# A decoder trunk on one core: GpSimd computes the low parts of 24 weight units beside the banded attention

## The chip, the cores and the metric

The kernel runs on one core of a Trainium2 chip. The metric is the device time of one launch in microseconds (us). Before the change it is 2423.09 us, the median of 3 runs (2422.06 to 2423.93).

The engines are named as in the profile: PE is TensorE, PEld its weight loads, DVE is VectorE, ACT is ScalarE, POOL is GpSimd, SP is SyncE, which issues the weight loads from memory.

## The reference, cut to what matters

Two decoder layers over 256 tokens of width 2048, in float32. Layer 0 begins with the banded grouped-query attention that the change is about:

```python
def swa_sink_attention(h, w_qkv, w_o, sinks):      # 32 heads of 64, 4 key/value heads, window 128
    q, k, v = split(h @ w_qkv)
    scores = q @ band(k).T * 64 ** -0.5 + alibi_bias, masked to the window
    probs = softmax(concat([scores, sink]))[..., :-1]
    return (probs @ band(v)) @ w_o

for i in range(2):
    h = h + (swa_sink_attention if i == 0 else diff_attention)(rmsnorm(h), ...)
    h = h + mem_cross_attention(rmsnorm(h), rmsnorm(mem), ...)
    h = h + conv_ffn(rmsnorm(h), ...)
return rmsnorm(h)
```

## The kernel before

**Weight units.** All weights stream through the core as 396 units of 512 x 512 numbers, numbered in the order of use. Unit u lies in slot u % 4. Four steps make it ready:

1. SP loads it into `raw` (1 MB); the load waits until the low part of unit u - 4 is done (`lo_ready`).
2. ACT rounds it to fp32r, the high part: `hi_unit`, L215, `whi <- raw`. It waits for the load and until PE has used unit u - 4 (`units_used`), and counts `hi_ready` up.
3. DVE subtracts, the low part: `lo_unit`, L223, `wlo <- raw - whi`. It waits for `hi_ready` and counts `lo_ready` up.
4. PE multiplies by both parts in three matmuls a tile (L309 to L311, `triple`), behind a wait for `lo_ready`, and counts `units_used` up.

`hi_unit` and `lo_unit` run AHEAD = 3 units before PE's use.

**The stage of the change** is `swa_group`, once for each of four groups g of 8 heads. B_SWA = 4, so the attention begins at unit 16. PE uses units 24 to 27 in group 0 (queries of the next group), 28 to 35 in group 1, 36 to 43 in group 2 (queries and output projection by turns), 44 to 47 in group 3 (output projection); the last output block follows with units 48 to 51 (`last_blocks`, and `final_blocks` on DVE and ACT). The high and low parts made in the stage are those of units 27 to 50.

Each engine's order is written out by hand, and each runs its own instructions in that order only. For one head j:

- PE: the scores (L611, L612); in groups 1 and 2 a unit behind every head's scores, in groups 0 and 3 behind those of odd heads only; then the transposes of the probabilities of head j - 1 (L621), then its products with the values for head j - 2 (L632 to L634).
- DVE: first `swa_normalize` of head j - 1 (L1489 sum, L1492 reciprocal, L1494 and L1495 scaling of the probabilities in `pbuf`), which waits for ACT's exponentials; then `swa_bias_max` of head j (L1474 bias, L1478 and L1479 maxima, L1482 negative maximum), which waits for PE's scores; then, where there is output projection, an addition to `h` (L373); then `lo_unit` of a coming unit: in groups 1 and 2 behind every head, in group 0 behind even heads, in group 3 behind odd ones.
- ACT: in the same rhythm first `hi_unit` (L215); in even heads from 4 on the copy of two heads' outputs (L1074); the exponentials of head j (L1063 to L1067), which wait for L1482; the copy of the transposed probabilities of head j - 1 (L1058).

At a group's end DVE also prepares the next group's keys, values, slopes and sinks (L1462 to L1466) and the low part of the outputs (L1500; in group 3 by halves, L1506, whose first half PE's L309 of the last block needs). GpSimd has no arithmetic in this kernel: it fills `ones` once and issues 14 small loads in the first 20 us.

Of the kernel before, what the change touches and what calls it, by code (L numbers as in the profile page):

```python
# [25 lines left out]
F32 = mybir.dt.float32  # L26
F32R = mybir.dt.float32r
ALU = mybir.AluOpType
# [25 lines left out]
SLOTS = 4  # L54
AHEAD = 3
# [3 lines left out]
B_SWA = B_MEM + 2 * DEPTH  # L59
# [3 lines left out]
B_X[1] = B_DIFF + 12 + 4  # L63
B_FF[1] = B_X[1] + 2
UNITS = 4 * (B_FF[1] + 3 * FF_STEPS)


X_MEM = [0, 1]
# [7 lines left out]
def trunk(nc, x, mem, norm_mix, norm_cross, norm_mem, norm_ffn, norm_final,  # L76
# [4 lines left out]
    with ExitStack() as ctx:  # L81
        def sb(name, shape, dt=F32):
            return ctx.enter_context(nc.sbuf_tensor(name, shape, dt))

        def sem(name):
            return ctx.enter_context(nc.semaphore(name))


        raw = sb("raw", [P, SLOTS, 4, 512])
        whi = sb("whi", [P, SLOTS, 4, 512], F32R)  # L90
        wlo = sb("wlo", [P, SLOTS, 4, 512], F32R)
# [67 lines left out]
        hi_ready = sem("hi_ready")  # L159
        lo_ready = sem("lo_ready")  # L160
# [46 lines left out]
        def hi_unit(act, b4, j):  # L207

            if isinstance(b4, int) and 4 * b4 + j >= UNITS:
                return  # L210
# [6 lines left out]
        def lo_unit(dve, b4, j):  # L217

            if isinstance(b4, int) and 4 * b4 + j >= UNITS:
                return  # L220
            s = j % SLOTS
            dve.wait_ge(hi_ready, b4 * 4 + j + 1)
            dve.tensor_tensor(wlo[:, s], raw[:, s], whi[:, s].bitcast(F32), ALU.subtract)\  # L223
               .then_inc(lo_ready, 1)
# [272 lines left out]

        @block.gpsimd
        def _(pool):
            pool.memset(ones[:], 1.0).then_inc(ones_ready, 1)  # L500

            pool.wait_ge(tokens_landed[1], 16)
            pool.dma_start(stage[0:16, P:2 * P], norm_final.rearrange("(c f) -> c f", f=P))\
                .then_inc(consts_landed, 16)
            for l in range(DEPTH):
                c0 = 256 + 4 * l * P
                pool.dma_start(stage[0:88, c0:c0 + 3 * P].rearrange("c (w f) -> c w f", w=3),
                              ffn_conv_w[l].rearrange("w (c f) -> c w f", f=P)).then_inc(consts_landed, 16)
                pool.dma_start(stage[0:88, c0 + 3 * P:c0 + 4 * P],
                              ffn_conv_b[l].rearrange("(c f) -> c f", f=P)).then_inc(consts_landed, 16)  # L510
            pool.dma_start(dist_swa[:], const_dist_swa).then_inc(consts_landed, 16)
            pool.dma_start(dist_diff[:], const_dist_diff).then_inc(consts_landed, 16)
            pool.dma_start(slopes[:], const_slopes).then_inc(consts_landed, 16)
            pool.dma_start(sinks[:], swa_sinks.broadcast_to([P, SWA_HEADS])).then_inc(consts_landed, 16)
            pool.dma_start(subln[:], diff_subln.rearrange("o n -> n o")).then_inc(consts_landed, 16)
            pool.dma_start(lamv[:, 0], diff_lambda_q1.broadcast_to([P, DIFF_DIM])).then_inc(consts_landed, 16)
            for i, a in enumerate((diff_lambda_k1, diff_lambda_q2, diff_lambda_k2)):
                pool.dma_start(lamv[:, 1 + i], a.broadcast_to([P, DIFF_DIM])).then_inc(lam_landed, 16)


        @block.tensor
# [837 lines left out]
        def _(dve):  # L1359
# [94 lines left out]
            def swa_queries(i, done):  # L1454

                dve.wait_ge(units_used, done)
                scaled_by_rstd(dve, q_sb[:, 2 * i:2 * i + 2], PA[:, 512 * i:512 * i + 512], 1,
                               SWA_DIM ** -0.5).then_inc(swa["q_evac"], 1)
# [9 lines left out]
            def swa_bias_max(g, j):  # L1468
                a = j % 2
                n = g * 8 + j  # L1470
                dve.wait_ge(swa["scores"], n + 1)
                if not isinstance(g, int) or 8 * g + j >= 2:
                    dve.wait_ge(swa["pT"], n - 1)
                dve.scalar_tensor_tensor(out=pbuf[:, a, 0:384], in0=dist_swa[:], scalar=slopes[:, j:j + 1],  # L1474
                                         in1=PC[:, 512 * a:512 * a + 384], op0=ALU.mult, op1=ALU.add)\
                   .then_inc(swa["biased"], 1)
                dve.wait_ge(swa["biased"], n + 1)
                dve.tensor_reduce(stat[:, a, 0, 0:1], pbuf[:, a, 0:P], AX_X, ALU.max)  # L1478
                dve.tensor_reduce(stat[:, a, 0, 1:2], pbuf[:, a, P:3 * P], AX_X, ALU.max)\  # L1479
                   .then_inc(swa["maxed"], 1)  # L1480
                dve.wait_ge(swa["maxed"], n + 1)
                dve.tensor_scalar(stat[:, a, 1, 0:2], stat[:, a, 0, 0:2], sinkg[:, j:j + 1], -1.0,  # L1482
                                  ALU.max, ALU.mult).then_inc(swa["negmax"], 1)

            def swa_normalize(g, j):
                a = j % 2
                n = g * 8 + j
                dve.wait_ge(swa["exped"], n + 1)
                dve.tensor_tensor(stat[:, a, 2, 0:2], stat[:, a, 2, 0:2], stat[:, a, 3, 0:2], ALU.add)\  # L1489
                   .then_inc(swa["summed"], 1)  # L1490
                dve.wait_ge(swa["summed"], n + 1)
                dve.reciprocal(stat[:, a, 4, 0:2], stat[:, a, 2, 0:2]).then_inc(swa["recips"], 1)  # L1492
                dve.wait_ge(swa["recips"], n + 1)
                dve.tensor_scalar(pbuf[:, a, 0:P], pbuf[:, a, 0:P], stat[:, a, 4, 0:1], None, ALU.mult)  # L1494
                dve.tensor_scalar(pbuf[:, a, P:3 * P], pbuf[:, a, P:3 * P], stat[:, a, 4, 1:2], None, ALU.mult)\  # L1495
                   .then_inc(swa["p_ready"], 1)

            def o_lo_all(s, g):
                dve.wait_ge(s["o_hi"], g + 1)
                dve.tensor_tensor(olo[:], o_sb, ohi[:].bitcast(F32), ALU.subtract).then_inc(s["o_lo"], 1)  # L1500

            def o_lo_half(s, i):

                part = slice(2 * i, 2 * i + 2)
                dve.wait_ge(s["o_hi"], GROUPS + i)
                dve.tensor_tensor(last_olo[:, part], o_sb[:, part], last_ohi[:, part].bitcast(F32),  # L1506
                                  ALU.subtract).then_inc(s["o_lo"], 1)

            def add_block(s, b4, j, src, nb):

                dve.wait_ge(units_used, b4 * 4 + j + 1)
                add_to_h(dve, src, nb).then_inc(s["h_added"], 1)

            def swa_group(g, with_q, with_o):
                b4 = g * 2 + (B_SWA + 1) if with_o else B_SWA + 2
                if with_o and not with_q:
                    b4 = B_SWA + 7
                src = [PB, PB, PB, PB] if with_q else [PA, PB, PA, PB]
                for j in range(8):
                    if j >= 1:  # L1520
                        swa_normalize(g, j - 1)
                    swa_bias_max(g, j)
                    if with_o and j >= 2 and j % 2 == 0:
                        add_block(swa, b4, j - 1 if with_q else j // 2 - 1, src[j // 2 - 1][:], j // 2 - 1)
                    if with_q and with_o:
                        lo_unit(dve, b4, j + AHEAD)
                    elif j % 2 == (0 if with_q else 1):
                        lo_unit(dve, b4, j // 2 + AHEAD)
                if with_q and with_o:
                    swa_queries(0, b4 * 4 + 7)  # L1530
                if not with_q:
                    o_lo_half(swa, 0)
                swa_normalize(g, 7)
                if not with_o:
                    swa_queries(0, b4 * 4 + 4)
                if with_o:
                    add_block(swa, b4, 7 if with_q else 3, src[3][:], 3)
                if with_q:
                    dve.wait_ge(swa["scores"], g * 8 + 8)
                    swa_queries(1, b4 * 4 + (7 if with_o else 4))  # L1540
                if with_q:
                    dve.wait_ge(swa["pv"], g * 8 + 8)
                    dve.wait_ge(swa["exped"], g * 8 + 8)
                    swa_prepare(g + 1)
                    o_lo_all(swa, g)
                else:
                    o_lo_half(swa, 1)
# [7 lines left out]
            with dve.Fori(1, 3) as g:  # L1555
                swa_group(g, True, True)
            swa_group(3, False, True)

            def add_wide(s, b4, j, p, nb, count):

# [298 lines left out]
            with dve.Fori(1, 3) as g:  # L1859
                b4 = g * 4 + (B_DIFF + 2)  # L1860
# [25 lines left out]
            b4 = B_DIFF + 14  # L1886
# [71 lines left out]
```

## Time and profile before

| | |
|---|---|
| median of 3 runs | 2423.09 us |
| the profiled execution, its own time | 2420.84 us |
| its span, first to last instruction | 2419.3 us |
| granted clock of TensorE, share of full speed | 0.996 |
| busy share PE / PEld / DVE / ACT / POOL | 98 / 88 / 75 / 49 / 0 % |
| low parts on DVE | 396 of 2288 ns, 904.9 us |
| the four groups of the stage, from and to | about 171 to 214, 214 to 278, 278 to 342, 342 to 394 us |

In rows of the trace, a start time in us from the span's start comes first, then a duration in us, the engine, the line, the operation and what it writes and reads. A bracket at the end is idle time of that engine just before, and who ended it.

### The profile page before, as it was taken

How to read it: one execution, taken by the hardware profiler on the slowest of the kernel's cores; microseconds unless marked ns; L12 is line 12 of the kernel's file. 1: busy time of each engine (PE TensorE's matmuls, PEld its weight loads, DVE VectorE, ACT ScalarE, POOL GpSimd, SP SyncE). 2: the span in 40 equal slices, each digit the busy share in tenths (PEclk: the TensorE clock that was granted, in tenths of full speed). 3: DMA queues.
4: the chain of work that ended last, by engine and by line, in shares of the span. 5: the costliest groups of instructions: out<-in, count | busy, mean ns of one | idle time of the engine just before them, and what ended most of it. 6: DMA issues, size and time to landing. Idle time of an engine off the chain costs nothing.

```text
span 2419.3 us, 37209 instructions
## 1 busy us (share of the span) xinstructions
PE 2372.3 (98%) x15166; PEld 2123.1 (88%) x15166; DVE 1805.5 (75%) x2160; ACT 1184.2 (49%) x1362; POOL 8.6 (0%) x19
## 2 busy tenths in 40 slices
PE   6999999999999999999999999999999999999998
PEld 6898889988888888888899989888888888888887
DVE  5766667768787777777966866788778787777777
ACT  5544446654444444444535444456544444444444
POOL 1000000000000000000000000000000000000000
PEclk9999999999999999999999999999999999999999
DMA  7653433465555555555464554434555555555551
GB/s 258 211 175 107 138 116 117 165 204 183 195 188 189 191 191 190 182 198 188 153 215 150 168 174 152 164 137 165 198 187 182 194 188 190 191 191 191 182 199 54
DMA packets 211818, 423.90 MB, mean 175 GB/s; under 512 B 6896, under 2 KB 7184, under 8 KB 211216
## 3 DMA queue, kind: packets, MB, share of 16 engines
q1 hardware_dynamic: 211152, 421.69, 52.1%
q0 software_dynamic: 576, 0.92, 0.2%
q8 instruction: 68, 1.11, 0.2%
q14 instruction: 22, 0.18, 0.0%
HBM read 420.48 MB, written 2.10 MB: 175 GB/s over the span
## 4 chain that ended last, share of the span: by engine, by line
PE 94%; DVE 4%; ACT 1%; DMA 1%; issue 0%; SPq 0%; DVEq 0%; ACTq 0%
PE pair L335 40%; PE pair L337 20%; PE pair L309 10%; PE pair L310 10%; PE pair L311 10%; DVE wlo L223 1%; PE pair L621 1%; PE pair L612 0%; PE pair L632 0%; PE pair L611 0%; DMA raw<-in_x_w_kv 0%; ACT whi L215 0%; DMA raw<-in_mem 0%; PE pair L633 0%; DVE h L1570 0%
## 5 line engine op out<-in xcount | busy, mean ns | idle before, releaser
L223 DVE TENSOR_TENSOR wlo<-raw,whi 128x2048 fp32r<-128x2048 f32 x396 | 904.9, 2288 | 297.5 <-ACT whi L215 297.2
L215 ACT ACTIVATE whi<-raw 128x2048 fp32r<-128x2048 f32 x396 | 756.7, 1913 | 686.8 <-PE pair L337 511.9
L335 PE MATMUL pair<-xx,whi 128*128 128x512 f32 x2944 | 1023.3, 394 | 0.0
L337 PE MATMUL pair<-xx,wlo 128*128 128x256 f32 x2944 | 816.3, 277 | 0.0
L335 PEld LDWEIGHTS pair<-xx,whi 128*128 128x128 f32 x2944 | 552.0, 188 | 129.0 <-issue 0.5
L337 PEld LDWEIGHTS pair<-xx,wlo 128*128 128x128 f32 x2944 | 552.8, 188 | 0.1
L335 PE MATMUL pair<-oo,whi 128*128 128x512 f32 x1280 | 445.1, 394 | 2.5 <-DVE h L1570 2.5
L337 PE MATMUL pair<-oo,wlo 128*128 128x256 f32 x1280 | 354.7, 277 | 0.0
L309 PE MATMUL pair<-xx,whi 128*128 128x256 f32 x1184 | 342.3, 289 | 10.9 <-DVE wlo L223 9.6
L310 PE MATMUL pair<-xx,whi 128*128 128x256 f32 x1184 | 335.9, 284 | 0.0
L311 PE MATMUL pair<-xx,wlo 128*128 128x256 f32 x1184 | 335.9, 284 | 0.0
L335 PEld LDWEIGHTS pair<-oo,whi 128*128 128x128 f32 x1280 | 240.0, 188 | 58.9 <-DVE h L1570 3.1
L309 PEld LDWEIGHTS pair<-xx,whi 128*128 128x128 f32 x1184 | 227.9, 193 | 21.2 <-issue 19.6
L337 PEld LDWEIGHTS pair<-oo,wlo 128*128 128x128 f32 x1280 | 240.3, 188 | 0.0
L310 PEld LDWEIGHTS pair<-xx,whi 128*128 128x128 f32 x1184 | 228.1, 193 | 1.2 <-issue 1.0
L311 PEld LDWEIGHTS pair<-xx,wlo 128*128 128x128 f32 x1184 | 228.0, 193 | 0.0
L309 PE MATMUL pair<-oo,whi 128*128 128x256 f32 x512 | 147.7, 288 | 1.0 <-DVE oo L1500 1.0
L1564 DVE TENSOR_TENSOR h<-h,pair 128x512 f32<-128x512 f32 x176 | 112.9, 683 | 43.2 <-PE pair L337 43.2
L311 PE MATMUL pair<-oo,wlo 128*128 128x256 f32 x512 | 144.9, 283 | 0.0
L310 PE MATMUL pair<-oo,whi 128*128 128x256 f32 x512 | 144.8, 283 | 0.0
L1672 DVE TENSOR_TENSOR work<-pair,work 128x512 f32<-128x512 f32 x88 | 56.7, 686 | 99.9 <-ACT work L1185 99.9
L1185 ACT ACTIVATE work<-pair 128x512 f32<-128x512 f32 x88 | 47.8, 595 | 149.6 <-PE pair L337 149.6
(197 smaller groups left out, 2205.6 us busy)
## 6 DMA issues: line engine op xcount, KB each, us to landing
raw<-in_ffn_w_up SPq DMA_DIRECT2D x176, 1024.0 KB, 5.0
raw<-in_ffn_w_down SPq DMA_DIRECT2D x88, 1024.0 KB, 5.0
raw<-in_diff_w_qkv SPq DMA_DIRECT2D x48, 1024.0 KB, 5.1
raw<-in_swa_w_qkv SPq DMA_DIRECT2D x20, 1024.0 KB, 5.1
raw<-in_x_w_kv SPq DMA_DIRECT2D x16, 1024.0 KB, 6.1
raw<-in_swa_w_o SPq DMA_DIRECT2D x16, 1024.0 KB, 5.1
raw<-in_diff_w_o SPq DMA_DIRECT2D x16, 1024.0 KB, 5.0
raw<-in_x_w_q SPq DMA_DIRECT2D x8, 1024.0 KB, 5.5
```

The costliest lines, as they stand in the source:

```text
L215: act.activation(whi[:, s], raw[:, s], ACT.Copy).then_inc(hi_ready, 1)
L223: dve.tensor_tensor(wlo[:, s], raw[:, s], whi[:, s].bitcast(F32), ALU.subtract)\
L309: pe.matmul(dst, ahi, bhi, start=start, stop=False, skip_group_check=True)
L310: pe.matmul(dst, ahi, blo, start=False, stop=False, skip_group_check=True)
L311: return pe.matmul(dst, alo, bhi, start=False, stop=stop, skip_group_check=True)
L335: pe.matmul(banks[m], whi[:, s, k, w], act2[:, c].rearrange("p a t -> p (a t)"), start=c == 0, stop=False, skip_group_check=True)
L337: ins = pe.matmul(banks[m][:, 0:SEQ], wlo[:, s, k, w], act2[:, c, 0], start=False, stop=last and k == 3, skip_group_check=True)
L621: ins = pe.transpose(pt_ps[:, dst_cols], src[:, src_cols], ident[:])
L1185: ins = act.activation(u_sb[:, 2 * i:2 * i + 2], src, ACT.Copy)
L1564: ins = dve.tensor_tensor(part, part, p[i][:].rearrange("p (m a t) -> p m a t", m=2, a=2)[:, :, 0], ALU.add)
L1672: ins = dve.tensor_tensor(part, high, part, ALU.add)
```

## The change

The 24 calls of `lo_unit` in DVE's `swa_group` are gone. GpSimd computes the same 24 low parts, each as soon as the high part is there. The first waits until DVE has done the low parts of all units before 27, which keeps the count `lo_ready` in order, and DVE waits for GpSimd's last one before it goes on with `final_blocks`. The tiles, the loads, and the orders of PE, ACT and SP stay as they are.

```diff
+SWA_UNITS = (4 * (B_SWA + 2) + AHEAD, 4 * (B_SWA + 8) + AHEAD)
...
         @block.gpsimd
         def _(pool):
+            def lo_unit_during_attention(u, j):
+                pool.wait_ge(hi_ready, u + 1)
+                pool.tensor_tensor(wlo[:, j], raw[:, j], whi[:, j].bitcast(F32), ALU.subtract)\
+                    .then_inc(lo_ready, 1)
+
...
+            pool.wait_ge(lo_ready, SWA_UNITS[0])
+            for u in range(*SWA_UNITS):
+                lo_unit_during_attention(u, u % SLOTS)
...
                     if with_o and j >= 2 and j % 2 == 0:
                         add_block(swa, b4, j - 1 if with_q else j // 2 - 1, src[j // 2 - 1][:], j // 2 - 1)
-                    if with_q and with_o:
-                        lo_unit(dve, b4, j + AHEAD)
-                    elif j % 2 == (0 if with_q else 1):
-                        lo_unit(dve, b4, j // 2 + AHEAD)
...
             swa_group(3, False, True)
+            dve.wait_ge(lo_ready, SWA_UNITS[1])
```

On DVE, the first head of group 0 before, from its bias to its probabilities; names are tiles, and in brackets stands what an instruction waits for:

```order
L1474 SCALAR_TENSOR_TENSOR pbuf<-dist_swa,slopes,pair 128x384 [waits swa_scores]
L1478 TENSOR_REDUCE stat<-pbuf 128x1 [waits swa_biased]
L1479 TENSOR_REDUCE stat<-pbuf 128x1
L1482 TENSOR_SCALAR stat<-stat,sinkg 128x2 [waits swa_maxed]
L223 TENSOR_TENSOR wlo<-raw,whi 128x2048 [waits hi_ready]
L1489 TENSOR_TENSOR stat<-stat 128x2 [waits swa_exped]
L1492 RECIPROCAL stat<-stat 128x2 [waits swa_summed]
L1494 TENSOR_SCALAR pbuf<-pbuf,stat 128x128 [waits swa_recips]
L1495 TENSOR_SCALAR pbuf<-pbuf,stat 128x256
```

The same place now (lines of the changed file are 11 higher here):

```order
L1485 SCALAR_TENSOR_TENSOR pbuf<-dist_swa,slopes,pair 128x384 [waits swa_scores]
L1489 TENSOR_REDUCE stat<-pbuf 128x1 [waits swa_biased]
L1490 TENSOR_REDUCE stat<-pbuf 128x1
L1493 TENSOR_SCALAR stat<-stat,sinkg 128x2 [waits swa_maxed]
L1500 TENSOR_TENSOR stat<-stat 128x2 [waits swa_exped]
L1503 RECIPROCAL stat<-stat 128x2 [waits swa_summed]
L1505 TENSOR_SCALAR pbuf<-pbuf,stat 128x128 [waits swa_recips]
L1506 TENSOR_SCALAR pbuf<-pbuf,stat 128x256
```

Nothing stands between the negative maximum and the sum any more; the low part has gone from DVE's row. This is the end of GpSimd's row, behind its last small load:

```order
L525 DMA lamv<-in_diff_lambda_k 128x64
L504 ISA
L504 TENSOR_TENSOR wlo<-raw,whi 128x2048 [waits hi_ready,lo_ready]
L504 TENSOR_TENSOR wlo<-raw,whi 128x2048 [waits hi_ready] x23
L83 UNCONDITIONAL_BRANCH
```

The 24 low parts stand there one behind the other, preceded by one instruction that the compiler adds. The rows of PE, ACT and SP hold the same instructions in the same order as before.

In this text lines have the numbers of the kernel before, for the changed kernel too.

## Rows read from the trace of the kernel before

**Rows 1.** The profile's part 1: busy us, share of the span, instructions

```profile
PE 2372.3 (98%) x15166; PEld 2123.1 (88%) x15166; DVE 1805.5 (75%) x2160; ACT 1184.2 (49%) x1362; POOL 8.6 (0%) x19
```

**Rows 2.** Windows of groups 0 and 1: width, busy PE, PEld, DVE, ACT, POOL, clock

```profile
171.00:214.00 43.00, 39.78 (x300) 34.44 (x296) 28.70 (x75) 22.64 (x59) 0.00 (x0) 1.00 0.35 117
214.00:278.00 64.00, 63.11 (x488) 57.88 (x488) 43.01 (x83) 30.02 (x62) 0.00 (x0) 1.00 0.41 132
```

**Rows 3.** Groups of DVE instructions, 165 to 394 us: busy us, mean ns

```profile
L223 DVE TENSOR_TENSOR wlo<-raw,whi 128x2048 fp32r<-128x2048 f32 x25 | 57.1, 2285 | 3.7 <-ACT whi L215 3.7
...
L1479 DVE TENSOR_REDUCE stat<-pbuf 128x1 f32<-128x256 f32 x32 | 13.1, 408 | 0.0
L1495 DVE TENSOR_SCALAR pbuf<-pbuf,stat 128x256 f32<-128x256 f32 x32 | 11.1, 348 | 0.0
L1494 DVE TENSOR_SCALAR pbuf<-pbuf,stat 128x128 f32<-128x128 f32 x32 | 9.2, 288 | 1.1
```

**Rows 4.** Timeline, group 0, heads 0 and 1

```profile
169.84 1.91 ACT L215 ACTIVATE whi<-raw 128x2048 fp32r<-128x2048 f32 x1 [3.84 <-PE pair L311]
171.65 0.61 DVE L1474 SCALAR_TENSOR_TENSOR pbuf<-dist_swa,slopes,pair 128x384 f32<-128x384 f32 x1 [0.42 <-PE pair L612]
...
172.94 0.23 DVE L1482 TENSOR_SCALAR stat<-stat,sinkg 128x2 f32<-128x2 f32 x1
...
175.28 0.16 DVE L1489 TENSOR_TENSOR stat<-stat 128x2 f32<-128x2 f32 x1
...
176.14 0.61 DVE L1474 SCALAR_TENSOR_TENSOR pbuf<-dist_swa,slopes,pair 128x384 f32<-128x384 f32 x1
...
179.90 0.55 PE L621 MATMUL pair<-ident,pbuf 128*128 128x128 f32 x3 [1.15 <-DVE pbuf L1495]
```

**Rows 5.** Timeline, group 0, between heads 3 and 4

```profile
188.78 1.90 ACT L215 ACTIVATE whi<-raw 128x2048 fp32r<-128x2048 f32 x1
189.94 0.55 PE L621 MATMUL pair<-ident,pbuf 128*128 128x128 f32 x3
...
190.59 0.38 ACT L1074 ACTIVATE work<-pair 128x256 f32<-128x256 f32 x1
...
191.11 0.40 PE L632 MATMUL pair<-ptbuf,work 128*64 128x128 f32 x2 [0.62 <-ACT work L1074]
```

**Rows 6.** Timeline, group 0, heads 6 and 7

```profile
199.50 1.90 ACT L215 ACTIVATE whi<-raw 128x2048 fp32r<-128x2048 f32 x1
...
202.05 0.23 DVE L1482 TENSOR_SCALAR stat<-stat,sinkg 128x2 f32<-128x2 f32 x1
...
210.52 0.55 PE L621 MATMUL pair<-ident,pbuf 128*128 128x128 f32 x3
```

**Rows 7.** Timeline, group 3, head 1

```profile
346.37 1.90 ACT L215 ACTIVATE whi<-raw 128x2048 fp32r<-128x2048 f32 x1
348.64 0.23 DVE L1482 TENSOR_SCALAR stat<-stat,sinkg 128x2 f32<-128x2 f32 x1
...
351.98 0.55 PE L621 MATMUL pair<-ident,pbuf 128*128 128x128 f32 x3 [0.92 <-DVE pbuf L1495]
```

**Rows 8.** Timeline, group 3, head 3

```profile
354.84 1.90 ACT L215 ACTIVATE whi<-raw 128x2048 fp32r<-128x2048 f32 x1
356.75 0.23 DVE L1482 TENSOR_SCALAR stat<-stat,sinkg 128x2 f32<-128x2 f32 x1
...
362.03 0.55 PE L621 MATMUL pair<-ident,pbuf 128*128 128x128 f32 x3
```

**Rows 9.** Timeline, end of group 3

```profile
379.45 0.68 DVE L1506 TENSOR_TENSOR xx<-work,xx 128x512 fp32r<-128x512 f32 x1
...
381.29 0.38 PE L309 MATMUL pair<-xx,whi 128*128 128x256 f32 x1
```

**Rows 10.** Groups of POOL instructions, whole span: busy us, mean ns

```profile
L500 POOL MEMSET ones<- 128x128 f32 x1 | 0.2, 205 | 0.3 <-POOLq L1947 0.3
L1947 POOL MEMSET const-float32-0.0<- 128x1 f32 x1 | 0.1, 99 | 0.3 <-issue 0.3
```

## The prediction

> **What bounds the kernel now.** I read the page's busy shares first: PE works for 98% of the span and DVE for 75% [rows 1]. So DVE's time counts only where PE stands still for it. The windows of the stage come next: in group 1 PE is busy for 63.11 of 64 us, while in group 0 it misses 3.2 us of 43 [rows 2]. Taking 24 x 2.285 = 54.8 us from DVE [rows 3] therefore cannot give 54.8 us back. The timeline shows what it can give: twice, at the opening of group 0 and of group 3, PE's transposes (L621) wait for the scaled probabilities (L1495) of head 1, 1.15 and 0.92 us [rows 4, 7]. Elsewhere in the two groups PE waits for ACT (0.62 us before L632) [rows 5] or for the group's preparation, which the change leaves alone.
>
> The reader should see the rhythm. From the bias of head 1 (176.14) to its transpose (179.90) pass 3.76 us; 1.29 of them lie before L1482 (171.65 to 172.94 in head 0) and 2.47 behind it [rows 4]. In groups 1 and 2 a head takes 64 / 8 = 8 us, and its probabilities are transposed only behind the next head's scores and unit, so 8 us of lateness are hidden there. In groups 0 and 3 every second head has no unit behind its scores, and the probabilities of the odd head before it are wanted almost at once. There the sum is made.
>
> **What the change does.** It removes 24 subtractions from DVE. Between L1482 and the sum (L1489) of a head with a unit, DVE spent 2.2 us on one; without it L1489 starts as soon as the exponentials are done, 1.47 us after L1482 (the 2.47 less about 1.0 from L1489 to the transpose, 0.86 of which lie between L1489 and the next bias, 175.28 to 176.14). In head 0 that is 172.94 + 1.47 = 174.4, not 175.28 [rows 4]: 0.9 us earlier. The same holds in group 3. Both places together would give PE 1.8 us, and no others wait for DVE's low part.
>
> It adds 24 subtractions on GpSimd, each starting when ACT's rounding ends. No row shows GpSimd at arithmetic. The lower bound is DVE's 2.29 us [rows 3]. For the upper one, a fill of 128 columns takes 205 ns and of one column 99 [rows 10], so 0.83 ns a column; three such passes over 2048 columns (two reads, a write) and 0.1 make 5.2 us. I take 4.6: twice DVE's time, since a slower engine that fetches its two operands in turn needs two of DVE's passes; it lies near the upper row, which is the only one of this engine. The Trainium skill (GPSIMD Engine Reference, section 3.1) gives 4497 ns for this size against 2293 ns on DVE; with it the sum below would be 0.8 us smaller, and the second figure agrees with DVE's row.
>
> Speed alone costs nothing: 4.6 us is less than a head's 8 us, PE needs a low part three units later, and the next load into the slot is wanted by ACT only after PE has used the unit, so these cover it. DVE's new wait in front of `final_blocks` is covered too: GpSimd's last unit starts near 377 and ends near 382, and DVE has work until then; behind the wait stand the additions to `h`, which wait for PE's last units.
>
> **The cost that decides is whether DVE can work while GpSimd does.** No row shows it: GpSimd is idle in every window. What speaks for trouble is the way DVE's small instructions reach SBUF. L1495 does 128 more columns than L1494 in 60 ns, 0.47 ns a column, where the subtraction needs 1.12 [rows 3]. So scaling uses two ways into SBUF at once, and a two-operand sum reads two tensors at once. If GpSimd's way is DVE's second, then an instruction of either kind (L1482, L1489, L1494, L1495, L1506) that comes while a 4.6 us subtraction runs stands until its end. The Trainium skill says just this (SBUF — State Buffer, "Who interferes with whom"): the pair of ports is locked for a whole instruction, and DVE instructions in a two-port mode or with two SBUF inputs contend with a GpSimd instruction that reads SBUF. By it the change costs time; without it, it gains 1.8 us. No run here has tested it. Against it stands that PE and ACT read SBUF beside DVE with no visible cost. I take the held case as likelier.
>
> **The sum, held case.**
> - Group 0, opening: the rounding ends at 171.75, GpSimd holds until 176.4. L1482, at 172.94 before, runs at 176.4. The next bias follows 2.35 behind it, at 178.75, and head 1's transpose 3.76 later, at 182.5 instead of 179.90 [rows 4]: +2.6.
> - Heads 2 and 3: exponentials of head 1 end at 181.5, a copy (0.4) and the rounding (1.9) follow, GpSimd works from 183.85 to 188.45. L1482 of head 2 comes at the same moment; I let it slip through. L1489 waits to 188.45, the bias of head 3 follows 0.86 later, its transpose at 193.05. PE wants it at 189.94 [rows 5] + 2.6 = 192.55: +0.5.
> - The next rounding follows head 3's exponentials, at 192.05 + 0.4, so the output copy L1074 starts at 194.3 instead of 190.59, and PE's L632 at 194.8 instead of 191.11 [rows 5]: 3.7 late, +0.6 more.
> - Heads 6 and 7: rounding ends at 201.40 + 3.7, GpSimd holds to 209.7. L1482 wanted 202.05 + 3.7, runs at 209.7; bias 212.05, transpose 215.8 against 210.52 + 3.7 = 214.2 [rows 6]: +1.6. Heads 4 and 5 fit.
> - Group 3, opening: rounding ends 348.27, GpSimd holds to 352.9; L1482 from 348.64 to there, transpose 2.47 later at 355.4 against 351.98 [rows 7]: +3.4.
> - Heads 3 and 5: rounding ends at 356.74 and L1482 starts at 356.75, so I let L1482 through; L1489 waits to 361.4, the transpose comes at 362.4 against 362.03 [rows 8]: +0.35 each.
> - The end: by the same pattern GpSimd's last unit ends 2.3 us behind the old start of L1506, 379.45; that takes 0.68, and PE's L309 wants it at 381.29 [rows 9]. 379.45 + 2.3 + 0.7 = 382.4: +1.1.
>
> Together 5.3 + 5.2 = 10.5 us. PE is the bound behind the stage too, so it is not given back. On the profiled execution's 2420.84 that makes 2431.3; the median stands 2.25 above that execution, so I forecast 2433.
>
> The bounds: with 2.29 us on GpSimd only the openings cost, 0.3 + 1.1, 2424.5. With 5.2 us each of the eight terms grows by 0.6: 15 us, 2438. If the coincidences (L1482 against GpSimd's start) all fall the other way, four terms grow by about 1.5: 17 us, 2440.
>
> **The rivals.**
> - *No interference* (the other side): DVE works beside GpSimd untouched, PE gets its 1.8 us, 2421.3, which a measurement can't tell from no change (0.2% is 4.8 us). It decides if L1482 to L1495 keep their distances while GpSimd works. For it speaks that nothing in the trace shows a hold. 0.27.
> - *Only two-operand instructions are held.* Then L1482 passes, and L1489 waits from 175.28 to 176.4 (+1.1), the later heads of group 0 add 1.0, group 3's opening 1.9 (352.9 less 351.0), the rest 1.8: 5.8 us, 2429. 0.12.
> - *GpSimd becomes the bound.* It needs over 8 us a unit in groups 1 and 2, at 12 us it falls behind by 16 x 4 = 64 us, of which three units ahead hide about 16: 2471. The upper row speaks against it. 0.05.
> - The held case has 0.56. That the change would not do what it says is excluded by the order of instructions.
>
> **How the numbers follow.** Nothing I found gives more than 1.8 us, so faster by over 0.2% has 0.03. Within 0.2% lie the rival without interference and the cheap ends of the others (a fast GpSimd): 0.34. Slower 0.63. The range reaches from the rival without interference to the lost coincidences, 2420.5 to 2440; outside stay the bound GpSimd, dearer holds and a larger gain, some 0.15. The likeliest case's own range is 2426 to 2440.
>
> **What would show it.** In the changed profile: GpSimd's low parts of about 4.6 us, start to start no nearer than a head; in group 0 head 0's L1482 or what follows it starting at GpSimd's end near 176.4, or right after the maxima if I am wrong; PE's waits for L1495 at the two openings grown to 3 to 4.5 us (held) or gone (free); groups 1 and 2 still 64 us each; no wait of DVE for `lo_ready` behind group 3. The prediction is wrong if DVE's instructions keep their starts while GpSimd works, if a GpSimd unit is near 2.3 us or above 8, or if GpSimd is the one that waits and DVE never does.

## The result and the profile after

The changed kernel takes 2439.22 us (median of 4 runs, 2435.65 to 2441.95) against 2422.57 us (4 runs). The ratio is 1.0072, 95% interval 1.006 to 1.0084: 17.4 us slower, between 14.5 and 20.4; the medians differ by 16.7. The forecast was 2433 us, with 10.5 us in its sum and a range up to 2440; 1.0072 times the 2423.09 it started from is 2440.5. One execution of e10, an experiment below, took 13357.5 us and is left out of its numbers.

Rows of the changed kernel and of the experiments have the line numbers of their own files. From the page of the changed kernel: the span, the busy shares, the start of the chain that ended last, by line, and the group of GpSimd's subtractions (out and in, count, busy us, mean ns).

```profile
span 2437.8 us, 37205 instructions
PE 2383.4 (98%) x15166; PEld 2132.1 (87%) x15166; DVE 1840.9 (76%) x2136; ACT 1182.4 (49%) x1362; POOL 119.0 (5%) x43
...
PE pair L337 39%; PE pair L339 20%; PE pair L311 10%; PE pair L312 10%; PE pair L313 10%; DVE wlo L225 1%; DVE stat L1493 1%; PE pair L632 1%; PE pair L623 0%; PE pair L622 0%; PE pair L643 0%; DMA raw<-in_x_w_kv 0%; DMA raw<-in_mem 0%; DVE h L1578 0%; DVE pbuf L1485 0%
...
L504 POOL TENSOR_TENSOR wlo<-raw,whi 128x2048 fp32r<-128x2048 f32 x24 | 110.4, 4599 | 268.9 <-ACT whi L217 268.9
```

DVE lost 24 subtractions of 2.29 us, 55 us, and yet is busy for 1840.9 us, where [rows 1] has 1805.5. The groups of DVE's instructions between 165 and 410 us tell where most of the missing 90 us came from. L1493 is the negative maximum (L1482 before), L1500 the sum (L1489), L1485 the bias (L1474), L1506 and L1505 the two scalings (L1495 and L1494).

```profile
L1493 DVE TENSOR_SCALAR stat<-stat,sinkg 128x2 f32<-128x2 f32 x32 | 66.0, 2062 | 1.1
L1500 DVE TENSOR_TENSOR stat<-stat 128x2 f32<-128x2 f32 x32 | 26.5, 828 | 27.2 <-ACT stat L1078 26.1
L1485 DVE SCALAR_TENSOR_TENSOR pbuf<-dist_swa,slopes,pair 128x384 f32<-128x384 f32 x32 | 19.5, 610 | 8.7 <-PE pair L623 8.7
L1506 DVE TENSOR_SCALAR pbuf<-pbuf,stat 128x256 f32<-128x256 f32 x32 | 15.6, 486 | 0.0
L1505 DVE TENSOR_SCALAR pbuf<-pbuf,stat 128x128 f32<-128x128 f32 x32 | 9.2, 287 | 1.1
```

The negative maximum takes 2062 ns on average, where it takes 229 in the kernel before. In all, L1493, L1500 and L1506 take 84.7 us more than the 7.3, 5.0 and 11.1 us of before. A held instruction is shown as a long one. In the stage 14 of L1493 and 7 of L1500 begin while a subtraction runs, and each of them ends 0.01 to 0.03 us behind that subtraction's end. The bias, with one operand from PSUM, keeps its 610 ns. The opening of group 0 in the order of time, which answers to [rows 4]:

```profile
170.20 1.91 ACT L217 ACTIVATE whi<-raw 128x2048 fp32r<-128x2048 f32 x1 [3.84 <-PE pair L313]
...
172.26 4.62 POOL L504 TENSOR_TENSOR wlo<-raw,whi 128x2048 fp32r<-128x2048 f32 x1 [153.30 <-ACT whi L217]
...
173.30 3.60 DVE L1493 TENSOR_SCALAR stat<-stat,sinkg 128x2 f32<-128x2 f32 x1
...
179.14 0.55 PE L632 MATMUL pair<-ident,pbuf 128*128 128x128 f32 x3 [1.22 <-DVE pbuf L1506]
...
181.76 0.16 DVE L1500 TENSOR_TENSOR stat<-stat 128x2 f32<-128x2 f32 x1 [1.24 <-ACT stat L1078]
```

The maximum starts at 173.30 and ends at 176.90, as the subtraction does (176.88). Head 1's transposes, which started at 179.90 [rows 4], start at 182.76. The opening of group 3, against [rows 7]:

```profile
357.40 4.54 POOL L504 TENSOR_TENSOR wlo<-raw,whi 128x2048 fp32r<-128x2048 f32 x1 [10.14 <-ACT whi L217]
357.71 4.25 DVE L1493 TENSOR_SCALAR stat<-stat,sinkg 128x2 f32<-128x2 f32 x1
...
364.20 0.90 PE L632 MATMUL pair<-ident,pbuf 128*128 128x128 f32 x3 [4.08 <-DVE pbuf L1506]
```

The maximum is held to 361.96; PE waits 4.08 us in place of 0.92. And the transposes themselves take 0.90 us in place of 0.55: PE has become slower. The windows show it (width, busy PE, PEld, DVE, ACT, POOL, then the granted clock, DMA share, GB/s):

```profile
182.00:184.00 2.00, 1.24 (x5) 0.91 (x6) 1.90 (x7) 1.90 (x2) 0.02 (x1) 0.51 0.03 8
184.00:192.00 8.00, 8.00 (x35) 7.02 (x34) 5.38 (x10) 2.72 (x11) 4.52 (x1) 0.50 0.26 77
360.00:364.00 4.00, 0.12 (x1) 0.00 (x0) 2.69 (x5) 1.55 (x6) 1.94 (x1) 0.87 0.17 32
364.00:372.00 8.00, 7.80 (x31) 6.49 (x32) 7.25 (x14) 3.35 (x7) 2.96 (x1) 0.50 0.30 115
```

In the course of both waits the granted clock falls, and TensorE runs for about ten microseconds at 0.50, its lower level of 1.2 GHz; both windows of [rows 2] have 1.00. For head 2's transposes, the next mark behind them, and for the first scores of group 3 the two kernels have these rows, first before, then after (with two more marks, of head 7 in group 0 and of the end of group 3):

```profile
187.87 0.49 PE L621 MATMUL pair<-ident,pbuf 128*128 128x128 f32 x3
...
341.90 0.50 PE L611 MATMUL pair<-work 64*128 64x128 f32 x4 [0.86 <-issue]
...
359.96 0.49 PE L621 MATMUL pair<-ident,pbuf 128*128 128x128 f32 x3
```

```profile
194.98 0.49 PE L632 MATMUL pair<-ident,pbuf 128*128 128x128 f32 x3
...
218.59 0.55 PE L632 MATMUL pair<-ident,pbuf 128*128 128x128 f32 x3
...
350.97 0.50 PE L622 MATMUL pair<-work 64*128 64x128 f32 x4 [0.85 <-issue]
...
376.17 0.49 PE L632 MATMUL pair<-ident,pbuf 128*128 128x128 f32 x3
...
398.84 0.39 PE L311 MATMUL pair<-xx,whi 128*128 128x256 f32 x1 [0.78 <-DVE xx L1517]
```

With them the whole loss can be laid out; each line is the lateness at a mark of PE's row, and what was added since the mark before:

| mark | before | after | late by | added, and by what |
|---|---|---|---|---|
| group 0, head 1 transposed | 179.90 | 182.76 | 2.86 | 0.35 from before the stage (the first bias at 172.00, not 171.65), 2.5 wait |
| head 2 | 187.87 | 194.98 | 7.11 | 4.25, the clock |
| head 7 | 210.52 | 218.59 | 8.07 | 0.96, waits of heads 5 and on |
| group 3, first scores | 341.90 | 350.97 | 9.07 | 1.0, groups 1 and 2 |
| head 1 transposed | 351.98 | 364.20 | 12.22 | 3.15, wait |
| head 2 | 359.96 | 376.17 | 16.21 | 4.0, the clock |
| end of group 3 | 381.29 | 398.84 | 17.55 | 1.3, waits |

The waits make 8.95 us, the clock 8.25. The rest of the kernel adds little: the spans differ by 18.5 us in these two executions.

The 1.0 us of groups 1 and 2 is nearly all one wait, at the end of group 1. The negative maximum of head 7 is held for 4.41 us, and behind this head no further scores follow in its group that would give PE work for the time:

```profile
277.12 4.41 DVE L1493 TENSOR_SCALAR stat<-stat,sinkg 128x2 f32<-128x2 f32 x1
```

```profile
283.77 0.55 PE L632 MATMUL pair<-ident,pbuf 128*128 128x128 f32 x3 [0.91 <-DVE pbuf L1506]
```

Two subtractions can also follow each other closely, and the second then holds another instruction of the same head. Here that cost nothing that PE's waits show, since the head's 8 us hide it:

```profile
239.78 4.60 POOL L504 TENSOR_TENSOR wlo<-raw,whi 128x2048 fp32r<-128x2048 f32 x1 [3.50 <-ACT whi L217]
239.84 1.22 DVE L375 TENSOR_TENSOR h<-h,pair 128x1024 f32<-128x1024 f32 x1
...
241.18 3.22 DVE L1500 TENSOR_TENSOR stat<-stat 128x2 f32<-128x2 f32 x1
...
244.83 4.78 DVE L1506 TENSOR_SCALAR pbuf<-pbuf,stat 128x256 f32<-128x256 f32 x1
244.85 4.61 POOL L504 TENSOR_TENSOR wlo<-raw,whi 128x2048 fp32r<-128x2048 f32 x1 [0.48 <-ACT whi L217]
```

Here too it is seen what is not held: the addition to `h` (L375), whose second operand is in PSUM, takes its 1.22 us in the middle of a subtraction.

### The profile page after: what moved, and what is told of

The parts are those of the page before. It is cut to its first block, busy times and chain, and to the rows that moved or that the text cites. A ratio compares the mean times of both kernels' runs of the same rounds, so it can differ in the third digit from the quotient of the medians.

```text
span 2437.8 us, 37205 instructions
## 1 busy us (share of the span) xinstructions
PE 2383.4 (98%) x15166; PEld 2132.1 (87%) x15166; DVE 1840.9 (76%) x2136; ACT 1182.4 (49%) x1362; POOL 119.0 (5%) x43
## 4 chain that ended last, share of the span: by engine, by line
PE 92%; DVE 5%; ACT 1%; DMA 1%; issue 1%; SPq 0%; DVEq 0%; ACTq 0%
PE pair L337 39%; PE pair L339 20%; PE pair L311 10%; PE pair L312 10%; PE pair L313 10%; DVE wlo L225 1%; DVE stat L1493 1%; PE pair L632 1%; PE pair L623 0%; PE pair L622 0%; PE pair L643 0%; DMA raw<-in_x_w_kv 0%; DMA raw<-in_mem 0%; DVE h L1578 0%; DVE pbuf L1485 0%
## 5 line engine op out<-in xcount | busy, mean ns | idle before, releaser
L225 DVE TENSOR_TENSOR wlo<-raw,whi 128x2048 fp32r<-128x2048 f32 x372 | 850.0, 2288 | 297.6 <-ACT whi L217 297.3
L504 POOL TENSOR_TENSOR wlo<-raw,whi 128x2048 fp32r<-128x2048 f32 x24 | 110.4, 4599 | 268.9 <-ACT whi L217 268.9
```

Source lines behind the costliest of these rows:

```text
L504: pool.tensor_tensor(wlo[:, j], raw[:, j], whi[:, j].bitcast(F32), ALU.subtract)\
```

## The experiments

Theory A: a GpSimd subtraction holds the DVE instructions that need GpSimd's way into SBUF, until its end; this costs time only where PE waits for an odd head's probabilities; and there it costs twice, since TensorE's clock falls when PE stands still. Rival B: any work on GpSimd costs its share. Rival C: the low clock comes from GpSimd's working beside TensorE. Ratios are to the kernel before, with 95% intervals; differences in us are those of the medians, by which the changed kernel is 16.7 us slower.

**e1: only groups 1 and 2 on GpSimd.**

```diff
-            for u in range(*SWA_UNITS):
+            pool.wait_ge(lo_ready, 31)
+            for u in range(31, 47):
...
+                    if with_q != with_o and j % 2 == (0 if with_q else 1):
...
+                        lo_unit(dve, b4, j // 2 + AHEAD)
```

> GpSimd does only the 16 units of groups 1 and 2 (31 to 46), DVE the other 8. Theory A (a GpSimd subtraction holds DVE's instructions, and it costs time only where PE waits for the odd head's probabilities, in groups 0 and 3, and there again through the clock): no change to the kernel before, within 2 us, at most the 1.0 us that groups 1 and 2 lost in the changed kernel; clock 0.996. Rival B (any subtraction on GpSimd costs its share, late low parts or a slower core): 16 of 24 units, so 16/24 of 17, 11 us slower.

Measured: 1.0006 (0.9996 to 1.0015), 1.9 us, not to be told from none. This fits A and not B. PE's wait at the end of group 1 is there again (0.91 us).

**e2: only groups 0 and 3 on GpSimd**, 8 units; DVE does the 16 in the middle.

```diff
+            for lo, hi in ((27, 31), (47, 51)):
+                pool.wait_ge(lo_ready, lo)
...
+                    if with_q and with_o:
+                        lo_unit(dve, b4, j + AHEAD)
```

> GpSimd does only the 8 units of groups 0 and 3, DVE the middle 16. Theory A: nearly the whole loss, 15 to 18 us slower than before, with both stretches at half clock. Rival B: 8/24 of 17, 6 us slower.

Measured: 1.006 (1.0043 to 1.0077), 15.5 us slower, granted clock 0.90 in group 0 (171 to 222 us) as in the changed kernel. A third of the units makes nearly all of the loss, as A says; B is out.

**e3: only the two openings back to DVE** (units 27 and 47), 22 units stay on GpSimd.

```diff
+            for lo, hi in ((28, 47), (48, 51)):
...
+                    if with_q != with_o and j == (0 if with_q else 1):
...
+                        lo_unit(dve, b4, AHEAD)
```

> Only the first unit of group 0 and the first of group 3 (27 and 47) go back to DVE; the other 22 stay on GpSimd. Theory A: the two waits of 2 to 4 us of PE at head 1 go, and the low clock behind them with them: 2 to 4 us slower than before, of 17. Rival B: 22/24 of 17 stay, 15 us. Rival C (the low clock comes from GpSimd's working beside TensorE, not from PE's standing still): the waits go, some 6 us, the clock stays low, 10 us slower.

Measured: 1.0017 (1.0008 to 1.0027), 4.6 us slower, a little above the 2 to 4 expected of A; the clock is 1.00 in every window from 171 to 420 us, and the waits for the probabilities are seven, none over 1.4 us. Two subtractions of 24 carry 12 of the 17 us. GpSimd works here nearly as much, at the same clock of TensorE as before.

**e4 and e8: idle matmuls in PE's waits.** e4 puts 5 in group 0 and 9 in group 3 ahead of head 1's transposes, into a piece of PSUM that nothing uses; e8 adds 3 ahead of head 0's in group 0. The output is unchanged.

```diff
+                    if j == 2 and with_q != with_o:
+                        for _ in range(5 if with_q else 9):
+                            pe.matmul(PD[:, 768:1024], ones[:], rstd[:, 1], start=True, stop=True)
```

> The changed kernel, with idle matmuls on PE into an unused piece of PSUM ahead of head 1's transposes: 5 in group 0, 9 in group 3, as long as the waits of 2.2 and 4.1 us there. The waits themselves stay. Theory A: the clock stays at full speed, 8 of the 17 us come back, 9 us slower than before. Rival C: the clock falls all the same, 17 us stay.

> As the run with idle matmuls, with three more of them in group 0 ahead of head 0's transposes (PE stands 1.2 us there). In the first run the clock fell in group 0 right behind the first wait, before the idle matmuls began, and held in group 3. Theory A: with this wait filled too the clock holds in group 0 as well, 8 to 10 us slower than before in place of 12.4. Rival C (GpSimd's work lowers it): it falls again at 180.

Measured: e4 1.0048 (1.0031 to 1.0065), 12.4 us slower; e8 1.0052 (1.0035 to 1.0069), 12.6 us slower. In time both fall short of what was expected of A, 9 us and 8 to 10 us, and e8 is no better than e4. The profiles show what the idle matmuls did to the clock. In group 3 both do what A says: head 1's transposes come at 362.80 in e8, where idle matmuls fill the wait, head 2's at 370.78, 7.98 us later as before the change (351.98 to 359.96), where the changed kernel takes 11.97. In group 0 e4's clock fell all the same, near 180.1: PE had stood for 1.22 us, and 0.4 us of idle matmuls had run. They went on at 0.50 and held up the transposes by some 1.7 us, and the clock fell once more at 207, so that e4 gained nothing in group 0. In e8, with the first wait filled as well, the clock held at 1.00 to 194 us. So a subtraction that runs beside TensorE doesn't lower the clock, and C is out. That e8 gained 4.1 us on the changed kernel's 16.7, and not 8.25, has two reasons. PE reached the next waits sooner, and the clock fell once more behind them (rows of e8: two of PE's waits, then the windows around them):

```profile
193.27 0.55 PE L632 MATMUL pair<-ident,pbuf 128*128 128x128 f32 x3 [0.19 <-DVE pbuf L1512]
194.82 0.40 PE L643 MATMUL pair<-ptbuf,work 128*64 128x128 f32 x2 [1.01 <-ACT work L1091]
```

```profile
192.00:194.00 2.00, 1.63 (x10) 0.83 (x7) 1.63 (x7) 2.00 (x4) 0.00 (x0) 1.00 0.67 260
194.00:196.00 2.00, 1.18 (x9) 1.04 (x10) 0.73 (x4) 1.99 (x8) 1.51 (x1) 0.97 0.00 0
196.00:198.00 2.00, 2.00 (x8) 1.35 (x8) 2.00 (x1) 0.23 (x1) 2.00 (x1) 0.50 0.00 0
```

And at the end of group 0 PE waited 1.34 us for held probabilities that it found ready in the changed kernel, where it came later.

**e11: the hold imitated without GpSimd.** The kernel before, where DVE does units 27 and 47 twice, ahead of L1482 in place of once behind it.

```diff
+                if isinstance(g, int) and (g, j) in ((0, 0), (3, 1)):
...
+                    for i in range(2):
+                        ins = dve.tensor_tensor(wlo[:, u % SLOTS], raw[:, u % SLOTS],
+                                                whi[:, u % SLOTS].bitcast(F32), ALU.subtract)
...
+                    ins.then_inc(lo_ready, 1)
                 dve.wait_ge(swa["maxed"], n + 1)
```

> The kernel before, without GpSimd. Only at the two openings DVE does the low part (units 27 and 47) twice, ahead of the negative maximum instead of once behind it, so that the maximum comes 4.6 us late, as when GpSimd holds it. Theory A (the clock follows PE's standing still): PE waits some 3 and 3 us more at the openings, the clock falls behind both and costs 4 us each: 12 to 15 us slower than before. Rival C (GpSimd's work lowers the clock): 6 us slower, clock at full speed behind the waits.

Measured: 2435.5 us, 1.0059 (1.0045 to 1.0073), 13.6 us slower with GpSimd idle. Windows of its group 0 and of group 3, then PE's wait in group 3:

```profile
180.00:184.00 4.00, 2.35 (x10) 1.52 (x9) 2.72 (x9) 3.73 (x10) 0.00 (x0) 0.50 0.19 72
184.00:188.00 4.00, 4.00 (x16) 3.02 (x15) 3.86 (x9) 1.10 (x5) 0.00 (x0) 0.50 0.23 24
...
364.00:368.00 4.00, 4.00 (x17) 3.35 (x17) 3.48 (x7) 2.94 (x6) 0.00 (x0) 0.50 0.00 0
```

```profile
361.01 0.90 PE L622 MATMUL pair<-ident,pbuf 128*128 128x128 f32 x3 [2.96 <-DVE pbuf L1506]
```

Being late at the two openings is enough to lose most of what the changed kernel lost, and the clock falls when PE stands still there, though GpSimd does nothing. In its profile the clock also falls at the start of group 3, as it does in e9 below, which adds no wait.

**e6: the maximum in two instructions of one column.**

```diff
-                dve.tensor_scalar(stat[:, a, 1, 0:2], stat[:, a, 0, 0:2], sinkg[:, j:j + 1], -1.0,
+                dve.tensor_scalar(stat[:, a, 1, 0:1], stat[:, a, 0, 0:1], sinkg[:, j:j + 1], -1.0,
+                                  ALU.max, ALU.mult)
+                dve.tensor_scalar(stat[:, a, 1, 1:2], stat[:, a, 0, 1:2], sinkg[:, j:j + 1], -1.0,
                                   ALU.max, ALU.mult).then_inc(swa["negmax"], 1)
```

> The changed kernel with DVE's negative maximum (one instruction of two columns) done as two instructions of one column. Theory A with the reason of the doubled rate (a tensor-scalar instruction is held because it takes two ways into SBUF, which it can't with one column): both pass while GpSimd works, with 0.15 to 0.25 us each, and the hold moves to the sum of two tensors behind them; the openings cost 1.1 and 1.9 us more than before in place of 2.5 and 3.2, so the clock may hold: 4 to 12 us slower than before. Theory E (any instruction that reads and writes SBUF through this form is held, whatever its width): the first of the two is held as the one was, 17 to 19 us slower.

Measured: 1.0042 (1.0026 to 1.0059), 9.7 us slower. In its first head both pass under the subtraction (171.08 to 175.70), and the sum behind them is held:

```profile
171.08 4.62 POOL L504 TENSOR_TENSOR wlo<-raw,whi 128x2048 fp32r<-128x2048 f32 x1 [152.23 <-ACT whi L217]
...
172.12 0.21 DVE L1493 TENSOR_SCALAR stat<-stat,sinkg 128x1 f32<-128x1 f32 x1
172.25 0.20 DVE L1495 TENSOR_SCALAR stat<-stat,sinkg 128x1 f32<-128x1 f32 x1
...
173.69 2.02 DVE L1502 TENSOR_TENSOR stat<-stat 128x2 f32<-128x2 f32 x1 [1.24 <-ACT stat L1078]
```

Over all 32 heads the one-column instructions take 214 and 204 ns on average. So theory E is out: the width decides. This fits the doubled rate, as the prediction argued it from L1494 and L1495, since a single column can't be shared between two ways; no row measures the rate of so small an instruction. PE's waits for the probabilities come to 4.2 us, 9.4 in the changed kernel and 2.1 before. The clock still fell at both openings (0.57 from 180 to 184 us, 0.50 from 358 to 362). The hope that it would hold there was wrong.

**e5: each low part in four GpSimd instructions.**

```diff
-                pool.tensor_tensor(wlo[:, j], raw[:, j], whi[:, j].bitcast(F32), ALU.subtract)\
+                for k in range(4):
+                    ins = pool.tensor_tensor(wlo[:, j, k], raw[:, j, k], whi[:, j, k].bitcast(F32),
...
```

> GpSimd makes each low part in four instructions of 512 columns in place of one of 2048. Theory A (a hold lasts to the end of the GpSimd instruction that runs): GpSimd works as long, but no DVE instruction is held over 1.2 us at a time; several of one head may be held in turn, by the next piece. Head 1's transposes come 1 to 3 us late in place of 2.5 and 4.1, the clock may still fall once: 4 to 12 us slower than before. Theory D (what holds DVE is GpSimd's being busy, until its queue is empty): as the changed kernel, 17 us.

Measured: 1.0025 (1.0013 to 1.0036), 6.7 us slower. GpSimd takes 5.0 us for the four, and three instructions of one head are held in turn, for about a piece each:

```profile
180.57 4.97 POOL L505 TENSOR_TENSOR wlo<-raw,whi 128x512 fp32r<-128x512 f32 x4 [5.24 <-ACT whi L217]
181.97 1.12 DVE L1502 TENSOR_TENSOR stat<-stat 128x2 f32<-128x2 f32 x1 [1.24 <-ACT stat L1080]
...
183.33 1.06 DVE L1507 TENSOR_SCALAR pbuf<-pbuf,stat 128x128 f32<-128x128 f32 x1
184.31 1.38 DVE L1508 TENSOR_SCALAR pbuf<-pbuf,stat 128x256 f32<-128x256 f32 x1
```

A hold ends with the instruction that runs, and the next one makes a new hold. Theory D, that the four pieces hold as one would, is out: each held instruction here waits for about one piece (1.24 us), not for four. PE waits 2.22 us ahead of head 1 in group 0, and the clock falls. In group 3 it waits longer, and in this profile the clock stays at 1.00:

```profile
357.35 0.55 PE L634 MATMUL pair<-ident,pbuf 128*128 128x128 f32 x3 [2.65 <-DVE pbuf L1508]
```

**e7 and e10: placed starts.** In e7 GpSimd still does all 24. In e10 it does 20, and DVE takes 29, 30, 49 and 50, so that GpSimd's do not queue in groups 0 and 3. The edit of e7:

```diff
+                if u in (27, 28):
+                    pool.wait_ge(swa["p_ready"], 4 + 2 * (u - 27))
+                if u == 29:
+                    pool.wait_ge(swa["o_lo"], 1)
+                if 47 <= u < 50:
+                    pool.wait_ge(swa["p_ready"], 28 + 2 * (u - 47))
```

> GpSimd still does all 24, but its starts are placed: units 27 and 28 wait until head 3's and head 5's probabilities are done, 29 until group 0's outputs are split, 47 to 49 until the probabilities of heads 3, 5 and 7 of group 3 are done. Theory A: the holds then fall where PE has slack, at most 0.5 us of new waiting, and both openings come 0.9 us earlier than before: 1 to 2 us faster than the kernel before, clock 0.996. Rival B: 24 units on GpSimd cost what they cost, 17 us slower; if the later low parts are what hurts, more than 17.

> As the run with placed starts, but without queues of GpSimd work: DVE does units 29, 30, 49 and 50 itself, GpSimd 27, 28, 47 and 48 at the placed times and 31 to 46 as they come. In the run with placed starts four subtractions back to back held four instructions of one head in turn, and PE waited 6.8 us. Theory A with one hold for each GpSimd instruction: the wait goes, what is left is the 1 to 2 us of groups 1 and 2, against which stand 0.9 us from each opening: within 2 us of the kernel before. Rival B: 20/24 of 17, 14 us slower.

Measured: e7 1.0047 (1.0031 to 1.0064), 10.4 us slower, a miss; e10 1.0005 (0.9995 to 1.0014), no difference. In e7 the waits at both openings are gone, and the clock is 1.00 in groups 0 and 3. But unit 29 was placed so late that four subtractions came in a row, and each held an instruction of one head, until PE stood for 6.8 us; the clock was 0.50 from 228 to 238 us. At the end of group 3 PE waited another 1.96 us, for GpSimd's low part itself. The first rows of the four:

```profile
214.23 18.16 POOL L504 TENSOR_TENSOR wlo<-raw,whi 128x2048 fp32r<-128x2048 f32 x4 [13.12 <-DVE oo L1517]
...
215.36 3.52 DVE L1499 TENSOR_SCALAR stat<-stat,sinkg 128x2 f32<-128x2 f32 x1
...
220.12 3.32 DVE L1506 TENSOR_TENSOR stat<-stat 128x2 f32<-128x2 f32 x1 [1.24 <-ACT stat L1084]
...
223.67 4.35 DVE L1511 TENSOR_SCALAR pbuf<-pbuf,stat 128x128 f32<-128x128 f32 x1
```

**e9: no GpSimd, another place on DVE**, behind the odd head's scaling.

```diff
+                    if with_q != with_o and j >= 2 and j % 2 == 0:
+                        lo_unit(dve, b4, j // 2 - 1 + AHEAD)
                     swa_bias_max(g, j)
...
```

> The kernel before, without GpSimd; in groups 0 and 3 DVE does the low part behind the odd head's scaling instead of behind the even (group 0) or odd (group 3) head's negative maximum. What PE waited for at the openings comes 0.9 us earlier each: PE's waits for L1495 (1.15 and 0.92 us) nearly gone, no new ones, 1 to 2 us faster than before, about as much as a measurement can tell. If the low parts' place matters otherwise (the later bias of even heads), no gain or 1 us slower.

Measured: 1.0000 (0.9991 to 1.0009). In the profile PE's waits for the probabilities, 2.1 us in all before, are one of 0.3 us:

```profile
PE pair L621 <- DVE pbuf L1495: 0.3, 1, 0.3
```

The span is 2417.0 us against 2419.3, but in this execution the stage itself begins 2.9 us earlier. Over its length e9 gains only 0.4 us, since its clock fell at the start of group 3 and cost 1.5 us (first scores to head 0's transposes 9.30 us, 7.82 before):

```profile
340.00:344.00 4.00, 3.89 (x21) 3.89 (x22) 2.62 (x10) 2.48 (x6) 0.00 (x0) 0.62 0.01 4
```

Ahead of it stand two waits of PE, 0.86 and 1.03 us, that all these kernels have. In the profiles of e2, e6, e9, e10 and e11 the clock falls behind them, in the other eight it doesn't. The timed runs see no gain of e9, and no version beats the kernel before by more than they can tell.

## Why the prediction was right and wrong

- **What bounds the kernel, and what DVE's freed time is worth.** Right: 55 us taken from DVE, at most 1.8 to be had, and e9 takes these waits away in the profile without a gain that the runs can tell.
- **GpSimd's time for a subtraction**, taken at 4.6 us: 4.60. The Trainium skill's 4497 ns (GPSIMD Engine Reference, section 3.1) is 2% short of it. The reason given, that it fetches its operands in turn, no run tests.
- **Whether DVE can work beside GpSimd.** Instructions of two kinds can't, as the likelier case had it; the reasons, the doubled rate and the two tensors in SBUF, fit e6 and the rows. The trace agrees with the Trainium skill (SBUF — State Buffer, "Who interferes with whom") at each point that it shows: 3.60, 3.22 and 4.78 us of hold to the end of the GpSimd instruction; none for the bias and the addition to `h` with an operand in PSUM, nor for the maxima (L1478 and L1479 keep their 0.29 and 0.41 us beside the first subtraction of the changed kernel).
- **The sum's terms for waits.** Right in place for groups 0 and 3. The openings came to 2.5 and 3.15 us, forecast 2.6 and 3.4. Group 0's others were 0.96 in place of 2.7: behind the slow clock PE came 4.25 us later and found most of them ready (in e8, where the clock held, it waited for head 3's probabilities and for L1074's copy, 0.19 and 1.01 us). The end of group 3 brought 1.3, forecast 1.8. Forecast as free and not free: groups 1 and 2, 1.0 us, since the last head of group 1 has no next scores to hide its hold. Nor do subtractions stay a head apart, as was expected: two started 5.07 us from each other. In all 8.95 for 10.5.
- **The step that failed: from the waits to the time, "Together 5.3 + 5.2 = 10.5 us".** The sum has waits of PE alone and counts each at its own length; it has no term for what TensorE's clock does when PE stands still. At each of the two openings the granted clock fell to 0.50 and the way to head 2's transposes took 4.25 and 4.0 us longer: 8.25 us, half of the loss. e3 took away the two waits and with them the low clock; e8 filled them and kept both openings at 1.00; e11 made the same low clock without GpSimd. The sentence behind the sum, that PE "is the bound behind the stage too, so it is not given back", held: 17.55 us late at the end of group 3, 18.5 at the end of the span. The rows of before, PE at 1.00 through the stage, with no wait over 1.2 us there, could have raised the question.
- **The range.** It ended at 2440, just under the 2440.5 that the ratio gives. That it comes so near is luck: its upper end was made of longer waits, and the waits came out shorter than in the sum.
- **The rivals.** No interference and only two-operand instructions held: both excluded by the rows above, the second by L1493, which is held with one operand. GpSimd as the bound: it waited 268.9 us for ACT, 153.3 of them ahead of its first subtraction, and took 4.6 us a unit. The direction stood on the likeliest case, and it was the right one.

What stays open: when a wait makes the clock fall. Each fall in the stage's profiles has waits of PE just ahead of it or around it (the least are 0.19 and 1.01 us, in e8), and filling the waits kept the clock up; but their length alone does not decide. The clock fell behind a single wait of 1.22 us (e4, group 0) and of 1.32 us (e6, group 3); it held behind 1.15 us before the change, 1.35 in e3 and 2.65 in e5; behind the same 0.86 and 1.03 us it fell in five profiles of thirteen. No run varied the length alone. So two single profiles can differ by a fall of 1.5 us or more that no edit made, and the timed runs have to decide.

## What to carry to other kernels

GpSimd beside a busy DVE is no free engine: one long two-operand instruction there held the DVE instructions that read two tensors from SBUF, and those of one tensor and two or more columns that scale or compare by a number, until its end, one for each GpSimd instruction. So a short chain of small instructions (a softmax) is bad company for it, and several GpSimd instructions in a row hold several links of the chain. Move such work only where the consumer has a whole GpSimd instruction of slack, place its start by a semaphore rather than as soon as it can, and cut it in pieces if it must overlap. And where TensorE is near 100% busy, a new wait can cost more than its length: here 2.5 and 3.15 us of new waiting brought some 4 us of low clock each. Look at the granted clock behind it, in more than one execution.

## What the runs showed of the hardware that was not expected

- At waits of 2.2 us (with one of 1.2 ahead of it) and 4.1 us TensorE's granted clock went from 1.00 to 0.50 for about ten microseconds, at a cost of 4.25 and 4.0 us; with the wait filled by idle matmuls, the same stretch of PE's work ran at 1.00 (7.98 us in place of 11.97).
- The same two waits of 0.86 and 1.03 us were followed by 0.50 in five profiles and not in eight others.
- A held DVE instruction is written down as a long one: 4.78 us for 256 columns that take 0.35.
- A queue of GpSimd instructions lets DVE have one instruction, or a few that need no second way, between two of them: four in a row (18.16 us) held four instructions of one head.
